# Two conditioning bursts in a row at the head of each pair, from two row buffers, in the first MLP

## The chip, the cores and the metric

The kernel runs on one core of one Trainium2 chip. The time is that of the device in microseconds, for the whole kernel; the number given for a kernel is the median of its runs. "Span" is the time from the first to the last instruction of one profiled execution.

## The reference

The kernel computes one inference step of a two-layer decoder trunk, in float32, for 256 prompt tokens and 8 x 8 sample tokens (320 token columns in all), with a model width of 2048. A layer is a mixer (attention with an RG-LRU in layer 0, a gated short convolution in layer 1) and a squared-ReLU MLP. Each of the four sublayers is modulated by its own conditioning vectors:

```python
def ada_modulate(c, w, b):
    m = jax.nn.silu(c) @ w + b
    shift, scale, gate = jnp.split(m[:, None, :], 3, axis=-1)
    return shift, scale, gate

def sq_relu_mlp(h, w1, w2):
    return jnp.square(jax.nn.relu(h @ w1)) @ w2
...
    shift, scale, gate = ada_modulate(c, W["ada_mlp_w"][layer], W["ada_mlp_b"][layer])
    h = modulated_norm(x, W["norm_mlp"][layer], shift, scale)
    x = x + gate * sq_relu_mlp(h, W["mlp_w1"][layer], W["mlp_w2"][layer])
```

W1 is 2048 x 8192 and W2 is 8192 x 2048; the conditioning matrices are 2048 x 6144 each and meet only nine rows of c. They are read from HBM once, as all weights are.

## The kernel before

Activations stay in SBUF, transposed: a tile is 128 channels x 320 tokens. Every large product is done with three float32r matmuls for each weight tile: a weight chunk (512 rows x 256 columns, 512 KB) is loaded into one of four slots of `raw` by SyncE (SP, `load`, L372), ScalarE copies it into `w_hi` (`split`, L588), VectorE subtracts that from it into `w_lo` (L966), and TensorE multiplies hi by hi, hi by lo and lo by hi (`mul` in `pair`; all its matmuls are recorded at L1656). A chunk is 24 matmuls. A pair is four chunks, which make two output tiles of 128 channels; pairs alternate between two PSUM banks. `w_hi` and `w_lo` have four slots too.

Three waits couple the chunks. Load k waits for `lo_ready` to reach k - 3, that is until chunk k - 4, the one that held its raw slot, has been split. The split of chunk k waits for `chunk_used` to reach k - 3, that is until chunk k - 4 has been multiplied. TensorE waits for `lo_ready` of its own chunk. So load k leaves when chunk k - 8 has been multiplied and chunk k - 4 split behind it. SP issues its DMAs in program order, and each waits in SP's queue behind those ahead of it.

The first MLP (layer 0) works in four blocks of 2048 hidden columns. A block has 8 pairs with W1 (h in, u out; the "column phase") and 8 pairs with W2 (u in, added to x). Between the chunks TensorE also works through conditioning matrices that later sublayers need, one "row" (128 rows x 2048 columns, 1 MB) at a time: a burst (`part_tile`) is four products of a 128 x 32 tile `cs` with a quarter of the row each, on four strips of the array, recorded as eight MATMULs of 128 x 512. In the five first turns of a block (a turn is two pairs: four turns with W1, one with W2) `turn_with_part` puts a burst ahead of chunks 0 and 2 of each pair, 4 to a turn and 80 in all. On SP's side the function of the same name issues, four times a turn, one row and two chunk loads:

```python
for n in range(4):
    sp.wait_ge(narrow_used, KN.now)
    sp.dma_start(narrow_row, ada_rows(ADA[a], row + P * n, part)).then_inc(narrow_in, 16)
    KN.up()
    for src in sources[2 * n:2 * n + 2]:
        load(src)
```

There is one row buffer, `narrow_row` (the tile `narrow`, L420 is its DMA), and `narrow_used` counts the bursts done, so a row is loaded when every burst before it is done. The first four chunks of a turn have been issued by the turn before, so the eight loads of a turn are those of its chunks 4 to 11. ScalarE and VectorE take the four splits of a pair and then that pair's output work (`relu` and square in the column phase, `residual` with W2), four chunks ahead of TensorE. The order of the DMAs and of the matmuls is written out by hand; only SP, ScalarE and VectorE use loops.

Of the kernel before, what the change touches and what calls it, by code (L numbers as in the profile page):

```python
# [13 lines left out]
P = 128  # L14
D = 2048
# [12 lines left out]
SLOTS = 4  # L28
COLS = 256
# [92 lines left out]
@contextmanager  # L122
def looped(eng, lo, hi, per):

    if hi - lo == 1:
        yield lo
        return
    before = [(t, t.base, t.off) for t in per]
    with eng.Fori(lo, hi) as i:
        for t, base, off in before:  # L130
            t.base, t.off = base + i * per[t], off - lo * per[t]
        yield i
    for t, base, off in before:
        added = t.off - (off - lo * per[t])
        assert added == per[t], f"a turn adds {added}, not {per[t]}"
        t.base, t.off = base, off + (hi - lo) * per[t]


def trunk_kernel(nc, A, O):
    with ExitStack() as ctx:  # L140
# [9 lines left out]
        def at(name, offset, shape, dt=F32):  # L150
            return nc.alloc_sbuf_tensor_at(name, shape, dt, offset=offset)

        def new(name, shape, dt=F32):
            return at(name, region(4 * int(np.prod(shape[1:]))), shape, dt)

        def sem(name):
            return ctx.enter_context(nc.semaphore(name))
# [5 lines left out]
        h_hi = at("h_hi", RH, [P, KT, T], F32R)  # L163
        h_lo = at("h_lo", RH + KT * TILE, [P, KT, T], F32R)
        RU = region(2 * KT * TILE)
        u_hi = at("u_hi", RU, [P, KT, T], F32R)
        u_lo = at("u_lo", RU + KT * TILE, [P, KT, T], F32R)
# [13 lines left out]
        RXP = region(4 * LT * (3 + SEQ))  # L181
# [2 lines left out]
        xl_s = at("xl_s", RXS, [P, LT, NB, 3 + DS])  # L184
        c_p = at("c_p", RXP, [P, 2, 2 + SEQ])
        c_s = at("c_s", RXS, [P, 2, NB, 2 + DS])
        h0 = new("h0", [P, LT, NB])
        sc_hist = new("sc_hist", [P, KT, NB, 2])
        lam4 = at("lam4", RH + 32768, [1, 4 * DH])
# [105 lines left out]
        wide_in = [sem(f"wide_in{s}") for s in range(WIDE)]  # L295
        first_in = [sem(f"first_in{s}") for s in range(FIRST)]
        first_used = sem("first_used")
        narrow_in = sem("narrow_in")
        wide_used, narrow_used = sems("wide_used narrow_used")
        amp_ready = sems("amp_ready")  # L300
        in_id, in_tab, in_far, in_c, in_rows = sems("in_id in_tab in_far in_c in_rows")
# [33 lines left out]
        def slab(W, row, col):  # L335

            def at_chunk(s):
                return W[row + 512 * s:row + 512 * (s + 1), bass.ds(col, COLS)].rearrange("(k p) n -> p k n", p=P)
            return at_chunk
# [9 lines left out]
        def ada_rows(W, row, part):  # L349

            return W[bass.ds(row, P), bass.ds(part * D, D)]
# [12 lines left out]
        def _(sp):  # L364
# [22 lines left out]
            def ada_wide(a, part):  # L387

                for n in range(KT):
# [3 lines left out]
                    sp.dma_start(wide_later[:, slot], ada_rows(ADA[a], P * n, part)).then_inc(wide_in[slot], 16)  # L393
                    KW.up()

            def ada_narrow(a, g, tiles):

                if not (isinstance(KN.now, int) and KN.now == 0):
                    sp.wait_ge(narrow_used, KN.now)
                sp.dma_start(narrow[:, :, :], ada_burst(ADA[a], tiles[0], g * GCOLS)).then_inc(narrow_in, 16)  # L400
                KN.up()
# [11 lines left out]
            def turn_with_part(src1, a, part, row, after):  # L413

                sources = [src1(s) for s in range(SLOTS)]
                if after is not None:
                    sources += [after(s) for s in range(SLOTS)]
# [6 lines that stand above are left out]
# [46 lines left out]
            def mlp_weights(layer):  # L470
                return A["mlp_w1"][layer], A["mlp_w2"][layer].rearrange("(b s k p) n -> b s p k n", b=BLOCKS, s=SLOTS, p=P)

            def inward(W2, b, j):
                return lambda s: W2[bass.ds(b, 1), s, :, :, bass.ds(j * COLS, COLS)].rearrange("o p k n -> p (o k) n")
# [8 lines left out]
            def feed_with_ada(b, a, part, after):  # L483

                W1, W2 = mlp_weights(0)
                with looped(sp, 0, 3, {K: 8, KN: 4}) as j:
                    turn_with_part(slab(W1, 0, b * D + j * (2 * COLS) + COLS), a, part, j * (4 * P),
                                   slab(W1, 0, b * D + (j + 1) * (2 * COLS)))
                turn_with_part(slab(W1, 0, b * D + 7 * COLS), a, part, 12 * P, inward(W2, b, 0))
                turn_with_part(inward(W2, b, 1), 2, 2, b * (4 * P), inward(W2, b, 2))  # L490
                with looped(sp, 3, KT // 2, {K: 4}) as j:
                    load_quad(inward(W2, b, j))
                if after is not None:
                    load_quad(slab(W1, 0, after))
# [1156 lines left out]
        def _(pe):  # L1651
# [6 lines left out]
            def pair(r, hi, lo, inputs=None, free=None, count=G, before=None, between=None):  # L1658

                pe.wait_ge(*(free or (pair_free, G.now + 1)))  # L1660
                for s in range(SLOTS):
                    slot = K.off % SLOTS
                    if before is not None:
                        before(s)
                    pe.wait_ge(lo_ready, K.now + 1)
                    for kk in range(4):
                        k = 4 * s + kk
                        if inputs is not None:
                            inputs(s, kk)
                        for m in range(2):  # L1670
                            out, cols = mm[:, r, m, 0:T], slice(P * m, P * m + P)
                            mul(out, w_hi[:, slot, kk, cols], hi[:, k, :], k == 0, False)
                            mul(out, w_hi[:, slot, kk, cols], lo[:, k, :], False, False)
                            ins = mul(out, w_lo[:, slot, kk, cols], hi[:, k, :], False, k == KT - 1)
                    ins.then_inc(chunk_used, 1)
                    K.up()
                    if between is not None:
                        between(s)
                count.up()
# [36 lines left out]
            def ada_wide():  # L1716
# [5 lines left out]
                part_tile(acc, k, wide_later[:, slot]).then_inc(wide_used, 1)  # L1722
                KW.up()

            def ada_part(bank, k):

                pe.wait_ge(narrow_in, KN.now * 16 + 16)
                part_tile(bank, k, narrow_row).then_inc(narrow_used, 1)
                KN.up()
# [21 lines left out]
            def turn_with_part(hi, lo, bank, first, inputs=None, free=(None, None), count=G, after=None):  # L1751

                def burst(first):
                    return lambda s: ada_part(bank, first + s // 2) if s % 2 == 0 else None

                pair(0, hi, lo, inputs, free[0], count, before=burst(first))
                pair(1, hi, lo, None, free[1]() if free[1] else None, count, before=burst(first + 2), between=after)

            def turn_with_ada(hi, lo, inputs=None, free=(None, None), count=G, after=None):

# [7 lines left out]
            def h_inputs(count):  # L1768

                def wait(s, kk):  # L1770
                    if s == 0 and kk < 3:
                        pe.wait_ge(h_ready, count + kk + 1)
                    elif kk == 0:
                        pe.wait_ge(h_ready, count + s + 3)
                return wait
# [32 lines left out]
            def turn(out, in_, rows=P):  # L1808
                return nc.tensor.transpose(out, in_, const[0:rows, 0:rows])  # L1809
# [256 lines left out]
            def u_block():  # L2066

                base, off = UB.base, UB.off
                UB.up(8)
                return lambda s, kk: pe.wait_ge(u_ready, base + (off + 2 * s + 2)) if kk == 0 else None  # L2070

            def mlp_with_parts(count):

                for b in range(BLOCKS):
                    pe.wait_ge(ada_turned, b + 4)
                    turn_with_part(h_hi, h_lo, acc, 0, h_inputs(count),
                                   ((pair_free, G.now + 1), lambda: (pair_free, G.now + 2)), R)
                    for i in range(1, 4):
                        turn_with_part(h_hi, h_lo, acc, 4 * i, None,
                                       ((relu_out, R.now - 1), lambda: (relu_out, R.now - 1)), R)  # L2080
                    relu = R.now
                    turn_with_part(u_hi, u_lo, acc_gate, 4 * b, u_block(),
                                   ((relu_out, relu - 1), lambda: (relu_out, relu)))
                    with looped(pe, 1, 4, {K: 8, G: 2}):
                        for r in range(2):
                            pair(r, u_hi, u_lo)
# [13 lines left out]
                            pair(r, u_hi, u_lo)  # L2100

            UB = Tally()
            pe.wait_ge(l_row, 1)
            norm()
            mlp_with_parts(10)
# [67 lines left out]
```

## Time and profile before

| | |
|---|---|
| median of 3 runs | 3166.12 us (3164.52 to 3168.07) |
| the profiled execution | 3169.29 us, span 3167.6 us |
| TensorE busy | 3061.3 us, 97% of the span |
| VectorE, ScalarE, GpSimd busy | 1480.2, 1084.5, 29.7 us |
| DMA | 624.90 MB, mean 197 GB/s |
| mean granted TensorE clock | 0.982 |

The first MLP goes from about 751 to 1758 us of the span. Busy time of TensorE is the union of its matmuls' records; matmuls overlap (one of 128 x 320 is recorded with 0.31 us), so the distance between starts tells what one costs. Times in the rows are microseconds from the start of the span.

### The profile page before, as it was taken

The numbers are of one execution on the slowest core, as the hardware profiler recorded it, in microseconds if no ns is written. First come the engines' busy times: TensorE is split into PE (matmuls) and PEld (weight loads), VectorE is DVE, ScalarE is ACT, GpSimd is POOL, SyncE is SP. The second block draws the span as 40 slices with busy tenths as digits, with TensorE's granted clock in tenths as the row PEclk, the third lists the DMA queues.
The fourth block names the chain that finished last, engine by engine and source line by source line (L and its number), as shares of the span: only waits on it lengthen the run. The fifth ranks groups of instructions, "written<-read, shape, count | busy, mean of one in ns | idle before, by whom it ended". The sixth has DMA issues, their size and how long they took to land.

```text
span 3167.6 us, 53269 instructions
## 1 busy us (share of the span) xinstructions
PE 3061.3 (97%) x21011; PEld 2818.3 (89%) x21011; DVE 1480.2 (47%) x2057; ACT 1084.5 (34%) x1309; POOL 29.7 (1%) x55
## 2 busy tenths in 40 slices
PE   7999987799999999999999999999999999999998
PEld 4888853598899899889889899999899999999998
DVE  3556544355344344334445644455544444444443
ACT  3334443234332332332332433333432333332332
POOL 0000000000000000000000000000000000000000
PEclk9999998899999999999999999999999999999999
DMA  9987789545765765775774344444444444444443
GB/s 329 335 274 239 240 345 390 221 142 178 251 216 181 263 227 172 252 247 160 245 262 150 123 150 145 152 148 147 125 151 147 144 149 150 143 151 142 147 152 106
DMA packets 451959, 624.90 MB, mean 197 GB/s; under 512 B 16960, under 2 KB 402753, under 8 KB 433028
## 3 DMA queue, kind: packets, MB, share of 16 engines
q1 hardware_dynamic: 443776, 595.65, 56.9%
q0 software_dynamic: 6112, 22.84, 1.9%
q10 hardware_dynamic: 1926, 4.24, 0.4%
q8 instruction: 119, 1.95, 0.3%
q14 instruction: 26, 0.21, 0.0%
HBM read 617.13 MB, written 5.54 MB: 197 GB/s over the span
## 4 chain that ended last, share of the span: by engine, by line
PE 92%; DMA 3%; DVE 2%; issue 2%; ACT 1%; POOL 0%; POOLq 0%; SPq 0%; ACTq 0%; DVEq 0%
PE mm L1656 86%; PE aux L1656 5%; DMA wide_later<-in_ada_mlp_w 2%; DMA wide_first<-in_ada_mix_w 1%; PE mm L1809 1%; DVE tmp L1047 1%; DVE h_lo L1073 0%; DMA kpage<-in_cache_k 0%; DVE tmp L1063 0%; DVE tmp L1066 0%; PE aux L2027 0%; DVE w_lo L966 0%; PE aux L1809 0%; ACT x_sq_b L661 0%; POOLq L542 0%
## 5 line engine op out<-in xcount | busy, mean ns | idle before, releaser
L966 DVE TENSOR_TENSOR w_lo<-raw,w_hi 128x1024 fp32r<-128x1024 f32 x752 | 919.4, 1225 | 1327.4 <-ACT w_hi L588 1325.8
L588 ACT ACTIVATE w_hi<-raw 128x1024 fp32r<-128x1024 f32 x752 | 795.1, 1059 | 1704.8 <-PE mm L1656 1704.8
L1656 PE MATMUL mm<-h_hi,w_hi 128*128 128x320 f32 x3712 | 1170.3, 315 | 30.6 <-DVE h_lo L1073 17.1
L1656 PE MATMUL mm<-h_hi,w_lo 128*128 128x320 f32 x3712 | 1154.7, 311 | 0.0
L1656 PE MATMUL mm<-h_lo,w_hi 128*128 128x320 f32 x3712 | 1154.7, 311 | 0.0
L1656 PEld LDWEIGHTS mm<-h_hi,w_hi 128*128 128x128 f32 x3712 | 704.0, 190 | 131.1 <-issue 102.2
L1656 PE MATMUL mm<-u_hi,w_hi 128*128 128x320 f32 x2304 | 713.7, 310 | 0.0
L1656 PE MATMUL mm<-u_hi,w_lo 128*128 128x320 f32 x2304 | 711.9, 309 | 0.0
L1656 PE MATMUL mm<-u_lo,w_hi 128*128 128x320 f32 x2304 | 711.9, 309 | 0.0
L1656 PEld LDWEIGHTS mm<-h_lo,w_hi 128*128 128x128 f32 x3712 | 704.9, 190 | 0.1
L1656 PEld LDWEIGHTS mm<-h_hi,w_lo 128*128 128x128 f32 x3712 | 704.3, 190 | 0.0
L1656 PEld LDWEIGHTS mm<-u_hi,w_hi 128*128 128x128 f32 x2304 | 432.5, 188 | 13.4 <-issue 13.4
L1656 PEld LDWEIGHTS mm<-u_lo,w_hi 128*128 128x128 f32 x2304 | 432.5, 188 | 0.0
L1656 PEld LDWEIGHTS mm<-u_hi,w_lo 128*128 128x128 f32 x2304 | 432.5, 188 | 0.0
L1656 PE MATMUL aux<-narrow,cs 128*32 128x512 f32 x792 | 112.3, 607 | 0.3 <-DMA narrow<-in_ada_mix_w 0.3
L1302 DVE TENSOR_TENSOR u_lo<-mtmp,u_hi 128x640 f32 x64 | 52.8, 826 | 67.0 <-ACT u_hi L730 67.0
L730 ACT ACTIVATE u_hi<-mtmp 128x640 f32 x64 | 47.3, 739 | 98.5 <-DVE mtmp L1299 98.5
L1237 DVE SCALAR_TENSOR_TENSOR xT<-mm,mod,xT 128x256 f32 (+1 forms) x160 | 69.4, 475 | 0.0
L1656 PE MATMUL aux<-wide_later,cs 128*32 128x512 f32 x384 | 55.7, 654 | 13.7 <-DMA wide_later<-in_ada_mlp_w 13.6
L1299 DVE TENSOR_TENSOR mtmp<-mtmp 128x640 f32<-128x640 f32 x64 | 52.4, 819 | 0.0
L1656 PE MATMUL aux<-wide_first,cs 128*32 128x512 f32 x232 | 43.3, 657 | 4.9 <-DMA wide_first<-in_ada_mix_w 4.1
L728 ACT ACTIVATE mtmp<-mm 128x640 f32<-128x640 f32 x64 | 44.0, 687 | 0.0
(278 smaller groups left out, 1063.4 us busy)
## 6 DMA issues: line engine op xcount, KB each, us to landing
raw<-in_mlp_w SPq DMA_DIRECT2D x512, 512.0 KB, 3.7
narrow<-in_ada_mlp_w SPq DMA_DIRECT2D x64, 1024.0 KB, 5.0
raw<-in_w_in_odd SPq DMA_DIRECT2D x96, 512.0 KB, 3.8
raw<-in_w_in_even SPq DMA_DIRECT2D x80, 512.0 KB, 6.5
narrow<-in_ada_mix_w SPq DMA_DIRECT2D x40, 1024.0 KB, 5.0
wide_later<-in_ada_mlp_w SPq DMA_DIRECT2D x32, 1024.0 KB, 9.8
wide_first<-in_ada_mix_w SPq DMA_DIRECT2D x58, 512.0 KB, 8.4
raw<-in_w_out_even SPq DMA_DIRECT2D x32, 512.0 KB, 3.6
```

The costliest lines, as they stand in the source:

```text
L588: fn(w_hi[:, slot], raw[:, slot], ACT.Copy).then_inc(hi_ready, 1)
L728: fn(mtmp[:, r], mm[:, r, :, 0:T], ACT.Relu).then_inc(relu_out, 1)
L730: fn(u_hi[:, bass.ds(j, 2), :], mtmp[:, r], ACT.Copy).then_inc(u_hi_ready, 1)
L966: v.tensor_tensor(w_lo[:, slot], raw[:, slot], w_hi[:, slot].bitcast(F32), ALU.subtract).then_inc(lo_ready, 1)
L1047: v.tensor_tensor(tmp4[:, first // 4 % 2, first % 4:first % 4 + count], xT[:, first:first + count, :], rstd[:, :].unsqueeze(1).broadcast_t ...
L1237: ins = v.scalar_tensor_tensor(x, mm[:, r, m, 0:SEQ], g, x, ALU.mult, ALU.add)
L1299: v.tensor_tensor(mtmp[:, r], mtmp[:, r], mtmp[:, r], ALU.mult).then_inc(u_val, 1)
L1302: v.tensor_tensor(u_lo[:, bass.ds(j, 2), :], mtmp[:, r], u_hi[:, bass.ds(j, 2), :].bitcast(F32), ALU.subtract).then_inc(u_ready, 1)
L1656: return nc.tensor.matmul(out, lhsT, rhs, start=first, stop=last)
L1809: return nc.tensor.transpose(out, in_, const[0:rows, 0:rows])
```

## The change

In the first MLP the bursts of a pair stand together ahead of its chunk 0, instead of one ahead of chunk 0 and one ahead of chunk 2. The first of the two reads `narrow_row`, the second a new buffer, `second_row`, of 8 KB a partition in the place of `xl_p` (whose readers are in the mixer before, and which the next mixer uses again for `c_p`), with a semaphore of its own. A row load now waits until all bursts but the last one ahead of it are done (`KN.now - 1`). The order of rows and chunk loads in SP's queue stays the same. Everything outside the first MLP is unchanged.

```diff
+        second_row = at("second_row", RXP, [P, D])[:, :]
...
-        narrow_in = sem("narrow_in")
+        narrow_in, second_in = sem("narrow_in"), sem("second_in")
...
+            def part_rows(W1_sources, a, part, row):
+
+                for n in range(4):
+                    sp.wait_ge(narrow_used, KN.now - 1)
+                    into, landed_in = ((narrow_row, narrow_in), (second_row, second_in))[n % 2]
+                    sp.dma_start(into, ada_rows(ADA[a], row + P * n, part)).then_inc(landed_in, 16)
+                    KN.up()
+                    for src in W1_sources[2 * n:2 * n + 2]:
+                        load(src)
...
-                    turn_with_part(slab(W1, 0, b * D + j * (2 * COLS) + COLS), a, part, j * (4 * P),
-                                   slab(W1, 0, b * D + (j + 1) * (2 * COLS)))
-                turn_with_part(slab(W1, 0, b * D + 7 * COLS), a, part, 12 * P, inward(W2, b, 0))
-                turn_with_part(inward(W2, b, 1), 2, 2, b * (4 * P), inward(W2, b, 2))
+                    turn(slab(W1, 0, b * D + j * (2 * COLS) + COLS), slab(W1, 0, b * D + (j + 1) * (2 * COLS)),
+                         a, part, j * (4 * P))
+                turn(slab(W1, 0, b * D + 7 * COLS), inward(W2, b, 0), a, part, 12 * P)
+                turn(inward(W2, b, 1), inward(W2, b, 2), 2, 2, b * (4 * P))
...
+            def ada_two(bank, k):
+
+                for n in range(2):
+                    pe.wait_ge((narrow_in, second_in)[n], 16 * (IN[n] + 1))
+                    part_tile(bank, k + n, (narrow_row, second_row)[n]).then_inc(narrow_used, 1)
+                    IN[n] += 1
...
+            def turn_with_two(hi, lo, bank, first, inputs=None, free=(None, None), count=G):
+
+                def burst(first):
+                    return lambda s: ada_two(bank, first) if s == 0 else None
+
+                pair(0, hi, lo, inputs, free[0], count, before=burst(first))
+                pair(1, hi, lo, None, free[1]() if free[1] else None, count, before=burst(first + 2))
...
-                    turn_with_part(h_hi, h_lo, acc, 0, h_inputs(count),
-                                   ((pair_free, G.now + 1), lambda: (pair_free, G.now + 2)), R)
+                    turn_with_two(h_hi, h_lo, acc, 0, h_inputs(count),
+                                  ((pair_free, G.now + 1), lambda: (pair_free, G.now + 2)), R)
```

The other calls in `mlp_with_parts` change in the same way.

## Rows read from the trace of the kernel before

**Rows 1.** The page: the chain that ended last, by engine.

```profile
PE 92%; DMA 3%; DVE 2%; issue 2%; ACT 1%; POOL 0%; POOLq 0%; SPq 0%; ACTq 0%; DVEq 0%
```

**Rows 2.** Busy time by window: late in the mixer, and a column phase.

```profile
core 0: us, PE busy (x) PEld busy (x) DVE busy (x) ACT busy (x) POOL busy (x), PEclk, DMA share, GB/s
560.00:640.00 80.00, 60.41 (x640) 42.20 (x639) 32.08 (x84) 23.51 (x51) 6.31 (x12) 0.84 0.54 205
1010.65:1134.05 123.40, 123.40 (x841) 107.93 (x841) 48.87 (x48) 41.17 (x45) 0.00 (x0) 1.00 0.76 256
```

**Rows 3.** Timeline of TensorE around a burst: start, duration, what, count.

```profile
1025.80 0.31 PE L1656 MATMUL mm<-h_hi,w_lo 128*128 128x320 f32 x1
1026.04 1.06 PE L1656 MATMUL aux<-narrow,cs 128*32 128x512 f32 x8
1027.03 0.41 PE L1656 MATMUL mm<-h_hi,w_hi 128*128 128x320 f32 x1
1027.28 0.30 PE L1656 MATMUL mm<-h_lo,w_hi 128*128 128x320 f32 x1
...
1030.65 0.31 PE L1656 MATMUL mm<-h_hi,w_hi 128*128 128x320 f32 x1
...
1034.26 0.64 PE L1656 MATMUL aux<-narrow,cs 128*32 128x512 f32 x4
```

**Rows 4.** Timeline of TensorE in the opening: sixteen burst matmuls together.

```profile
92.78 0.31 PE L1656 MATMUL mm<-h_hi,w_lo 128*128 128x320 f32 x1
93.02 0.62 PE L1656 MATMUL aux<-wide_first,cs 128*32 128x512 f32 x2
...
94.87 0.42 PE L1656 MATMUL mm<-h_hi,w_hi 128*128 128x320 f32 x1
95.12 0.31 PE L1656 MATMUL mm<-h_lo,w_hi 128*128 128x320 f32 x1
```

**Rows 5.** Timeline of SP's queue in the column phase: a row, two chunk loads.

```profile
1019.16 0.35 SPq L420 DMA_DIRECT2D narrow<-in_ada_mlp_w  x1
1019.82 0.99 SPq L372 DMA_DIRECT2D raw<-in_mlp_w  x2
```

**Rows 6.** Timelines of ScalarE, VectorE and SP around two splits.

```profile
1030.85 1.06 ACT L588 ACTIVATE w_hi<-raw 128x1024 fp32r<-128x1024 f32 x1 [0.72 <-PE mm L1656]
1031.94 1.23 DVE L966 TENSOR_TENSOR w_lo<-raw,w_hi 128x1024 fp32r<-128x1024 f32 x1 [0.80 <-ACT w_hi L588]
1003.74 1.23 DVE L966 TENSOR_TENSOR w_lo<-raw,w_hi 128x1024 fp32r<-128x1024 f32 x1 [2.29 <-ACT w_hi L588]
1005.13 0.37 SPq L372 DMA_DIRECT2D raw<-in_mlp_w  x1
```

**Rows 7.** A row issued behind a raw load, twice; landings of 75 rows.

```profile
737.41 0.37 SPq L372 DMA_DIRECT2D raw<-in_mlp_w  x1
738.15 0.36 SPq L420 DMA_DIRECT2D narrow<-in_ada_mix_w  x1
...
narrow<-in_ada_mix_w SPq DMA_DIRECT2D x1, 1024.0 KB, 5.4
...
1496.18 0.37 SPq L372 DMA_DIRECT2D raw<-in_mlp_w  x1
1497.07 0.34 SPq L420 DMA_DIRECT2D narrow<-in_ada_mlp_w  x1
...
narrow<-in_ada_mlp_w SPq DMA_DIRECT2D x1, 1024.0 KB, 5.7
...
DMA to landing us min/median/max: 4.8/5.0/7.4
```

**Rows 8.** Timelines of TensorE, VectorE and SP in the MLP's first turn.

```profile
768.64 0.64 PE L1656 MATMUL aux<-narrow,cs 128*32 128x512 f32 x4
...
777.02 1.06 PE L1656 MATMUL aux<-narrow,cs 128*32 128x512 f32 x8
...
772.27 3.65 DVE L966 TENSOR_TENSOR w_lo<-raw,w_hi 128x1024 fp32r<-128x1024 f32 x3
...
773.68 1.83 SPq L372 DMA_DIRECT2D raw<-in_mlp_w  x2
```

More of the change, by code:

```diff
@@ L485, in feed_with_ada, with turn @@
                 W1, W2 = mlp_weights(0)
+                def turn(first, second, *where):
+                    part_rows([f(s) for f in (first, second) for s in range(SLOTS)], *where)
                 with looped(sp, 0, 3, {K: 8, KN: 4}) as j:
-                    turn_with_part(slab(W1, 0, b * D + j * (2 * COLS) + COLS), a, part, j * (4 * P),
-                                   slab(W1, 0, b * D + (j + 1) * (2 * COLS)))
-                turn_with_part(slab(W1, 0, b * D + 7 * COLS), a, part, 12 * P, inward(W2, b, 0))
-                turn_with_part(inward(W2, b, 1), 2, 2, b * (4 * P), inward(W2, b, 2))
+                    turn(slab(W1, 0, b * D + j * (2 * COLS) + COLS), slab(W1, 0, b * D + (j + 1) * (2 * COLS)),
+                         a, part, j * (4 * P))
+                turn(slab(W1, 0, b * D + 7 * COLS), inward(W2, b, 0), a, part, 12 * P)
+                turn(inward(W2, b, 1), inward(W2, b, 2), 2, 2, b * (4 * P))
                 with looped(sp, 3, KT // 2, {K: 4}) as j:
@@ L2075, in mlp_with_parts @@
                     pe.wait_ge(ada_turned, b + 4)
-                    turn_with_part(h_hi, h_lo, acc, 0, h_inputs(count),
-                                   ((pair_free, G.now + 1), lambda: (pair_free, G.now + 2)), R)
+                    turn_with_two(h_hi, h_lo, acc, 0, h_inputs(count),
+                                  ((pair_free, G.now + 1), lambda: (pair_free, G.now + 2)), R)
                     for i in range(1, 4):
-                        turn_with_part(h_hi, h_lo, acc, 4 * i, None,
-                                       ((relu_out, R.now - 1), lambda: (relu_out, R.now - 1)), R)
+                        turn_with_two(h_hi, h_lo, acc, 4 * i, None,
+                                      ((relu_out, R.now - 1), lambda: (relu_out, R.now - 1)), R)
                     relu = R.now
-                    turn_with_part(u_hi, u_lo, acc_gate, 4 * b, u_block(),
-                                   ((relu_out, relu - 1), lambda: (relu_out, relu)))
+                    turn_with_two(u_hi, u_lo, acc_gate, 4 * b, u_block(),
+                                  ((relu_out, relu - 1), lambda: (relu_out, relu)))
                     with looped(pe, 1, 4, {K: 8, G: 2}):
@@ L2102, in _ @@
             UB = Tally()
+            IN = [KN.now, 0]
             pe.wait_ge(l_row, 1)
```

## The prediction

> **What bounds the kernel.** I read the page first, for who sets the end. The chain that ended last is TensorE for 92% of the span [rows 1], so a change counts only by what it adds to or takes from TensorE's own sequence. Next the windows: in a column phase of the first MLP (1010.65 to 1134.05) TensorE is busy for all of 123.40 us at a granted clock of 1.00, while the DMA engines are busy for 0.76 of it and move 256 GB/s [rows 2]. So TensorE waits for nothing there now. Then TensorE's timeline, for what one burst costs, and the timelines of SyncE, ScalarE and VectorE, for when the row that a burst needs can be on its way. I count the chunks of a turn from 0 to 7; a pair is four chunks, and the heads are chunks 0 and 4.
>
> **What a burst costs now.** The last matmul before a burst starts at 1025.80, the burst's eight at 1026.04, the next chunk's first matmul at 1027.03 and its second at 1027.28 [rows 3]. The burst itself takes 0.99. Plain matmuls follow each other every 0.147 (23 of the 24 of chunk 1027.03, less the first step of 0.25, reach to 1030.65). So a burst adds 1.23 - 0.15 on the way in and through, and 0.10 on the way out: 1.19. A half pair, from one burst to the next, is 1034.26 - 1026.04 = 8.22, or 8.227 as the mean of the 15 in the 123.40 us of [rows 2]; a pair of four chunks is 16.45.
>
> **What two in a row cost.** The trace has no two row bursts between chunks, but in the opening twice as many burst matmuls stand together: from the last plain matmul at 92.78 to the next at 94.87 is 2.09, again with 0.25 to the one after it [rows 4]. Two bursts apart take 2 x 1.19 = 2.38; together 2.09 - 0.15 + 0.10 = 2.04. One entry, drain and exit less: 0.34. There is one such merge a pair, 4 blocks x 5 turns x 2 pairs = 40, so 13 to 14 us less, if both rows lie in the buffers when TensorE comes to the head. The number of burst matmuls, row bytes and waits stays as it is; the new buffer lies over xl_p, whose last use is before this MLP, so it costs nothing.
>
> **When the second row is there.** This decides the sign. SP's order does not change: row 0, loads 4 and 5, row 1, loads 6 and 7, row 2, loads 8 and 9, row 3, loads 10 and 11. What changes is the wait ahead of a row. Before, rows 1 and 3 wait for the burst just done at chunk 0 or 4, and are wanted two chunks later; SP's row goes out first and its two chunk loads behind it (1019.16, then 1019.82 [rows 5]), it lands in a median of 5.0 [rows 7], and 8.22 - 1.34 = 6.9 are there for it (SP issued at 1019.16 for the burst at 1026.04). After, the wait of row 3 (for burst 1) is long met, but the row stands in SP's queue behind load 9. Load 9 waits until chunk 5 has been split, since it reuses that raw slot, and the split of chunk 5 waits for chunk 1 to be used, since it reuses that slot of w_hi. So row 3 can't leave before chunk 2 has begun and a split is done, and it is wanted at chunk 4. Row 1 stands in the same way behind load 5. Rows 0 and 2 have twice the time and aren't late.
>
> From the first matmul s of a chunk without a burst ahead: it is 1030.65, w_hi starts at 1030.85 and w_lo ends at 1031.94 + 1.23 = 1033.17 [rows 3, 6], that is s + 2.52. SP issues the raw load 0.16 after the end of w_lo (1003.74 + 1.23 to 1005.13 [rows 6]): s + 2.68. The row follows some 0.65 later, the step between two issues in [rows 5], and moves behind half its size in raw. The nearest rows are the places where a row was issued right behind a raw load: 737.41 and 738.15 with 5.4 to landing, so 6.1 after the raw issue; 1496.18 and 1497.07 with 5.7, so 6.6 [rows 7]. (Two more such places give 6.7 and 8.9, with longer steps between the issues.) I take 6.35, since the step will be short as in the first but some rows land late: up to 7.4 where the median is 5.0 [rows 7]. The second burst can start at s + 2.68 + 6.35 + 0.04 (from a landing to the matmul that waits for it, as the chain has it in the mixer) = s + 9.07.
>
> Without a wait it would start at s + 7.04 (48 matmuls of 0.147) + 0.09 (way in) + 0.86 (half of the growth from one burst of 0.99 to 1.85 for two, 94.87 - 93.02 [rows 4]) = s + 7.99. So TensorE waits 1.1 us between the two bursts of a head. The pair then lasts 3.62 + 3.52 to s, 9.07 to the second burst, and 0.99 for it: 17.20 against 16.45. **Each pair gets 0.75 longer, not 0.34 shorter.** Bounds by the rows: 6.1 gives +0.50 a pair, 6.6 gives +1.00. The same holds in the turn of W2, where VectorE's residual work stands at the heads and not where chunk 5 is split.
>
> A page would put it elsewhere. The Trainium skill (DMA: Bandwidth & Descriptors, Anatomy of one DMA) fits a transfer as 2.0 us plus its bytes at 436 GB/s, for loads issued from GpSimd. An estimate from that fit for raw and row together is 5.6 after the raw issue, which makes a pair 16.45, no change. The trace speaks against it: a row alone lands after 5.0 [rows 7] where the fit has 4.4.
>
> **The first turn.** At the first head nothing is late: the norm keeps TensorE until h is ready, load 5 was issued by 745, long before, and both bursts of that head lie in the norm's wait. But the norm also delays the splits of chunks 4 to 6: VectorE does them in one go from 772.27, SP issues loads 8 and 9 at 773.68 and 774.8, and row 3 leaves at about 775.6 [rows 8]. Behind two raw loads it lands at 780.6 (5.0) to 782.6; I take 782. TensorE, which leaves out the burst at 768.64, is at the head by 775.7 and gets on at 783, where before it was there at 777.02 + 0.99 = 778.0 [rows 8]. That is +5 (3.6 to 5.6).
>
> **The sum.** 40 heads: the first free, the second +5, 38 x 0.75 = 28.5; together +33.5, against the profiled execution's own 3169.3 (span 3167.6 and 1.7 around it): 3202.8. That execution is 3.2 above the median of the three runs, 3166.1, so the forecast is 3166.1 + 33.5 = 3199.6, rounded 3199. The bounds: 38 x 0.50 + 4 = +23 and 38 x 1.00 + 6 = +44, so 3189 to 3210.
>
> **The rivals.**
> (a) Faster: the second row is hidden, and what is left is the merge. 40 x 0.34 = 13.6, and the second burst of the first head goes into the norm's wait, 0.85 more: 3166.1 - 14.4 = 3152. For it: DMA is busy 0.76 [rows 2], so bandwidth is there. It decides from where raw and row together land within 5.3 of the raw issue (7.99 - 2.68); no row shows less than 6.1. Chance 0.08.
> (b) No change to be measured: the row overlaps the raw load more than it did at 738.15, and lands 5.5 to 5.8 after the raw issue, the wait eating just what the merge gives. 38 x 0 + 4.5 gives 3170. Chance 0.09. The page's fit would be this case.
> (c) Worse than forecast: TensorE, which now stands still for 1 us in 17, is granted a lower clock. Where it stood still for a quarter of the time the grant was 0.84 [rows 2]. If 0.95 were granted over the some 680 us of the turns, that is 34 us more: 3233. Against it: TensorE would still be busy for 94% of each pair. Chance 0.05.
> The forecast has the remaining 0.78. What a measurement of this kernel can tell from no change is about 0.2%, 6 us. Faster 0.08, same 0.09, slower 0.83.
>
> **Range.** The forecast's own is 3189 to 3210. To hold 8 in 10 I reach down to (b), 3169, and up to 3211.
>
> **What would show it.** In the profile after: TensorE's burst rows narrow and second_row next to each other at each head; an idle time of about 1 us ahead of the second_row matmuls, ended by the DMA of second_row, 39 times; pairs of 17.2 in the chain; issues of second_row right behind a raw load, 5.5 to 6 to landing, while those of narrow leave earlier than they need; clock 1.00 as before; nothing changed before 750, and the second MLP only shifted. The step of the first head shows as 5 us lost by 783. The prediction is wrong if second_row lands before TensorE has done the first burst, if the raw load ahead of it leaves before the split that I put ahead of it, or if the merged bursts cost more than 2.04.

## The result, and the profile after

The changed kernel takes 3220.98 us (median of 4 runs, 3216.62 to 3231.18) against 3166.43 for the kernel before: a ratio of 1.0177, 95% interval 1.0164 to 1.019. That is 54.6 us slower. The sign and the mechanism are as forecast, the size isn't: 33.5 was forecast, and the time lies 10 us above the range. The profiled execution is the slowest of the four, 3231.18, with a span of 3229.5, so 61.9 us are to be found in its trace.

The page after. First the shares of the engines, the chain that ended last (by engine and by line, two lines) and the group of the second bursts (count | busy, mean ns | idle time ahead of them and its releaser):

```profile
PE 3070.7 (95%) x21011; PEld 2825.3 (87%) x21011; DVE 1480.7 (46%) x2057; ACT 1085.0 (34%) x1309; POOL 29.8 (1%) x55
...
PE 80%; DMA 10%; DVE 4%; issue 2%; ACT 2%; SPq 1%; POOL 0%; POOLq 0%; DVEq 0%; ACTq 0%
PE mm L1671 75%; DMA second_row<-in_ada_mlp_w 5%; PE aux L1671 4%; DMA second_row<-in_ada_mix_w 3%; DVE w_lo L981 2%; DMA wide_later<-in_ada_mlp_w 1%; ACT w_hi L603 1%; DMA wide_first<-in_ada_mix_w 1%; PE mm L1839 1%; SPq L373 1%; DVE tmp L1062 1%; DVE h_lo L1088 0%; DMA kpage<-in_cache_k 0%; DVE tmp L1078 0%; DVE tmp L1081 0%
...
L1671 PE MATMUL aux<-second_row,cs 128*32 128x512 f32 x256 | 37.5, 661 | 45.7 <-DMA second_row<-in_ada_mlp_w 33.2
```

Before, TensorE held 92% of the chain [rows 1]; now it holds 80%, and the chain goes through the second row's DMA and what stands ahead of that DMA: SP's queue, w_lo and w_hi. The DMA queues move the same 624.90 MB as before, at 193 GB/s in place of 197: the row's transfer is not more work, it is late.

An ordinary head, in TensorE's timeline (to be set against [rows 3]), then SP's queue and VectorE's split ahead of it, and the two transfers with their time to landing:

```profile
1593.21 1.06 PE L1671 MATMUL aux<-narrow,cs 128*32 128x512 f32 x8
1595.23 1.06 PE L1671 MATMUL aux<-second_row,cs 128*32 128x512 f32 x8 [0.96 <-DMA second_row<-in_ada_mlp_w]
1596.22 0.41 PE L1671 MATMUL mm<-h_hi,w_hi 128*128 128x320 f32 x1
...
1610.50 0.64 PE L1671 MATMUL aux<-narrow,cs 128*32 128x512 f32 x4
```
```profile
1587.37 1.23 DVE L981 TENSOR_TENSOR w_lo<-raw,w_hi 128x1024 fp32r<-128x1024 f32 x1 [2.29 <-ACT w_hi L603]
...
1588.75 0.37 SPq L373 DMA_DIRECT2D raw<-in_mlp_w  x1
1589.39 0.34 SPq L402 DMA_DIRECT2D second_row<-in_ada_mlp_w  x1
...
second_row<-in_ada_mlp_w SPq DMA_DIRECT2D x1, 1024.0 KB, 5.8
```

The load leaves 0.15 after the end of w_lo (1587.37 + 1.23), the row 0.64 behind it, and it lands 6.4 after the load's issue, at 1595.2. TensorE has been at the head since 1593.21 and starts the second burst 0.04 after the landing. The pair lasts 1610.50 - 1593.21 = 17.29; 17.20 was forecast.

A late head, in the same view; then the windows before the wait ends, behind it and later (length, busy times, PEclk, DMA share, GB/s):

```profile
1627.75 1.07 PE L1671 MATMUL aux<-narrow,cs 128*32 128x512 f32 x8
1632.47 1.94 PE L1671 MATMUL aux<-second_row,cs 128*32 128x512 f32 x8 [3.65 <-DMA second_row<-in_ada_mlp_w]
1634.33 0.63 PE L1671 MATMUL mm<-h_hi,w_hi 128*128 128x320 f32 x1
1634.77 0.47 PE L1671 MATMUL mm<-h_lo,w_hi 128*128 128x320 f32 x1
1635.03 0.47 PE L1671 MATMUL mm<-h_hi,w_lo 128*128 128x320 f32 x1
```
```profile
1627.50:1632.40 4.90, 1.31 (x11) 0.21 (x9) 2.36 (x3) 2.38 (x3) 0.00 (x0) 0.93 0.85 270
1632.47:1638.40 5.93, 5.93 (x23) 4.27 (x24) 0.35 (x1) 0.00 (x0) 0.00 (x0) 0.50 0.70 259
1638.69:1644.00 5.31, 5.31 (x39) 5.31 (x38) 1.23 (x1) 1.48 (x2) 0.00 (x0) 1.00 0.06 13
```

This row landed 8.5 after its issue, not 5.8. TensorE stood still for 3.65 us, and then the granted clock was 0.50, the lower of its two levels (1.2 GHz): the burst takes 1.86 to the next matmul in place of 0.99, plain matmuls step by 0.27 in place of 0.147, until 1638.5. This pair lasts 22.77.

**The balance** of the 61.9 us, from the starts of the 80 bursts in TensorE's timeline. The second burst starts 0.88 after the first where its row is there (as in e2 below, which never waits). At 39 heads, all but the first, it starts later: at 27 of them 1.86 after, on the mean, and at 12 between 2.2 and 5.7. All that is over 0.88 sums to 60.1. Behind eight of these 12 the clock fell, after stops of 1.89 to 4.65 us; what their pairs last beyond the wait, 1.4 to 2.8 each, sums to 15.3. Merging gives back 39 x (16.453 - 16.127) = 12.7, the pair of the kernel before less that of e2. Together +62.7, 0.8 more than the 61.9; that rest isn't assigned.

### The profile page after: what moved, and what is told of

The parts are those of the page before. It is cut to its first block, busy times and chain, and to the rows that moved or that the text cites. A ratio compares the mean times of both kernels' runs of the same rounds, so it can differ in the third digit from the quotient of the medians.

```text
span 3229.5 us, 53269 instructions
## 1 busy us (share of the span) xinstructions
PE 3070.7 (95%) x21011; PEld 2825.3 (87%) x21011; DVE 1480.7 (46%) x2057; ACT 1085.0 (34%) x1309; POOL 29.8 (1%) x55
## 2 busy tenths in 40 slices
DMA packets 451959, 624.90 MB, mean 193 GB/s; under 512 B 16960, under 2 KB 402753, under 8 KB 433028
## 4 chain that ended last, share of the span: by engine, by line
PE 80%; DMA 10%; DVE 4%; issue 2%; ACT 2%; SPq 1%; POOL 0%; POOLq 0%; DVEq 0%; ACTq 0%
PE mm L1671 75%; DMA second_row<-in_ada_mlp_w 5%; PE aux L1671 4%; DMA second_row<-in_ada_mix_w 3%; DVE w_lo L981 2%; DMA wide_later<-in_ada_mlp_w 1%; ACT w_hi L603 1%; DMA wide_first<-in_ada_mix_w 1%; PE mm L1839 1%; SPq L373 1%; DVE tmp L1062 1%; DVE h_lo L1088 0%; DMA kpage<-in_cache_k 0%; DVE tmp L1078 0%; DVE tmp L1081 0%
## 5 line engine op out<-in xcount | busy, mean ns | idle before, releaser
L1671 PE MATMUL mm<-h_hi,w_hi 128*128 128x320 f32 x3712 | 1169.6, 315 | 29.2 <-DVE h_lo L1088 16.7
L1671 PE MATMUL aux<-second_row,cs 128*32 128x512 f32 x256 | 37.5, 661 | 45.7 <-DMA second_row<-in_ada_mlp_w 33.2
L1671 PE MATMUL aux<-narrow,cs 128*32 128x512 f32 x536 | 79.6, 611 | 0.3 <-DMA narrow<-in_ada_mix_w 0.3
```

Source lines behind the costliest of these rows:

```text
L1671: return nc.tensor.matmul(out, lhsT, rhs, start=first, stop=last)
```

## The experiments

Each is the changed kernel with an edit. Its ratio is to runs of the kernel before on the same chip.

**1. The row one load earlier (e1), both rows ahead of all loads (e2).** Only the order in SP's queue changes.

```diff
-                for n in range(4):
+                for n, (lo, hi) in enumerate(((0, 1), (1, 4), (4, 5), (5, 8))):   # e1
+                for n, (lo, hi) in enumerate(((0, 0), (0, 4), (4, 4), (4, 8))):   # e2
...
-                    for src in W1_sources[2 * n:2 * n + 2]:
+                    for src in W1_sources[lo:hi]:
                         load(src)
```

> The changed kernel, but in SyncE's queue rows 1 and 3 stand one load earlier, behind loads 4 and 8 instead of 5 and 9. If the loss comes from the row standing behind a load that waits for the split of chunk 1 (or 5), the row now leaves one chunk (3.5 us) earlier and lands some 2.5 us before it is wanted: the waits of about 2.0 us from the first to the second burst shrink to 0.86, the pair lasts 16.1, and what is left is the merge, 40 x 0.34 less, with some 3 us lost at the second head, where loads are late after the norm: about 3155 us. Rival, that two bursts together or the second buffer itself cost time: it stays near 3215. Rival, that the DMA engines have no room for it: between the two.

> The changed kernel with both rows of a head issued together, ahead of the four chunk loads of a pair. By the theory of the queue no row is late, the second head neither: 3166 - 40 x 0.34 - 0.85 = 3152 us, in all heads 1.85 us from the first burst to the next chunk. Rival, that 2 MB at once hold back the chunk loads: waits of TensorE for w_lo appear, and the time is above 3160. Rival, that merging saves nothing: 3165.

e1: 3156.52 us, ratio 0.997 (0.996 to 0.9979). e2: 3153.01, ratio 0.9957 (0.9944 to 0.9971), 12.5 below the 3165.49 of the runs of before beside it. A head of e2 in TensorE's timeline, and SP's queue of the pair:

```profile
1581.08 1.06 PE L1671 MATMUL aux<-narrow,cs 128*32 128x512 f32 x8
1581.96 1.04 PE L1671 MATMUL aux<-second_row,cs 128*32 128x512 f32 x8
1582.93 0.42 PE L1671 MATMUL mm<-h_hi,w_hi 128*128 128x320 f32 x1
...
1597.20 0.64 PE L1671 MATMUL aux<-narrow,cs 128*32 128x512 f32 x4
```
```profile
1584.31 0.35 SPq L402 DMA_DIRECT2D narrow<-in_ada_mlp_w  x1
1584.71 0.42 SPq L402 DMA_DIRECT2D second_row<-in_ada_mlp_w  x1
1589.09 10.99 SPq L373 DMA_DIRECT2D raw<-in_mlp_w  x4
```

Two bursts take 1582.93 - 1581.08 = 1.85, as in the opening [rows 4], and the pair 16.12 (16.13 on the mean of the heads). Both rows of the next head have left 12 us before it. So the merge is worth what was forecast of it, and the change loses by the place of row 1 and row 3 in the queue against the burst that needs them. In e1, 4 of 39 heads still wait, 0.4 to 2.2 us each; in e2 none does.

**2. The bursts apart again, with everything else of the change (e3), and together at chunk 2 (e4).** `ada_one` is one burst of `ada_two`, with that burst's own buffer and semaphore.

```diff
-                    return lambda s: ada_two(bank, first) if s == 0 else None
+                    return lambda s: ada_one(bank, first + s // 2, s // 2) if s % 2 == 0 else None   # e3
+                    return lambda s: ada_two(bank, first) if s == 2 else None                        # e4
```

> The changed kernel with its two buffers, its semaphores and its order in SyncE's queue, but the bursts stand apart again, ahead of chunks 0 and 2 of a pair. Row 1 leaves as late as in the changed kernel but is wanted two chunks later. By the theory that only the place of the second burst against its row's landing costs: the time of the kernel before, 3166 us, with no wait for a row. Rival, that the shared place in memory, the late issue or the other wait cost by themselves: well above 3170.

> The changed kernel with both bursts together ahead of chunk 2 of each pair instead of chunk 0, with SyncE's order unchanged. Row 1 then has two chunks (7 us) more. By the theory: no wait for a row, the merge's gain of 40 x 0.34 = 13.6 us, less 1.2 because the norm hides no burst any more: 3154 us. Rival, that standing together costs: above 3166.

e3: 3162.98 us, ratio 0.9993 (0.9984 to 1.0002), no change that can be told. So the buffer in the place of xl_p, the semaphores, the wait and the late issue cost nothing that can be told as long as the burst that needs the row stands two chunks later. e4: 3152.75, ratio 0.996 (0.9945 to 0.9975): standing together at a place where the row is there gives the whole gain, with SP's order untouched. Neither kernel's waits name a row's DMA in this MLP.

**3. Half of each second row (e5), and the row ahead of its load (e7).** These divide the row's lateness.

```diff
+                    width = (D, D // 2)[n % 2]                                        # e5
+                    sp.dma_start(into[:, 0:width], ADA[a][bass.ds(row + P * n, P), bass.ds(part * D, width)]).then_inc(landed_in, 16)
...
+                for n, (lo, hi) in enumerate(((0, 1), (1, 4), (4, 5), (5, 8))):       # e7
+                    if n % 2:
+                        sp.wait_ge(lo_ready, K.now - 3)
+                    else:
+                        sp.wait_ge(narrow_used, KN.now - 1)
```

> The changed kernel with half of each second row: its DMA brings 128 rows x 1024 columns (512 KB), and the burst multiplies those columns twice, so the conditioning values that come from the second rows are not the reference's; TensorE's matmuls keep their number and size. If the row is late because it moves behind a raw load and takes its own 1 MB, it lands about 1.4 us earlier, so the second burst starts some 0.86 after the first at most heads and the pair lasts 16.1: 40 x 0.34 less, with some us left at late landings and at the second head, about 3157 us. Rival, that a late start alone sets it (the fixed part of a transfer): the wait stays above 0.5 us and the time above 3180.

> The changed kernel, but rows 1 and 3 change places with the load that stands ahead of them (5 and 9) and wait for the same split as that load, so a row leaves at the moment at which load 5 left. This divides the lateness into the wait for the split (kept) and the standing behind a raw load (0.65 us of issue and that load's transfer, gone). By the theory the row lands 5.0 after an issue at s + 2.68, so it is there at s + 7.7, just before s + 8.0: no wait at most heads, waits of 1 to 3 us where a row lands late, some 3 us at the second head; 3166 - 12.7 + about 10 = 3163 us. Rival, that the split's wait alone makes it late: nearly the changed kernel's 3215.

e5: 3166.7 us, ratio 1.0005 (0.9995 to 1.0014). e7: 3166.07, ratio 0.9998 (0.9984 to 1.0012). Time to landing of second_row (min/median/max), of e5 and then of e7; after the change it was 5.4/5.8/8.5:

```profile
DMA to landing us min/median/max: 4.1/4.8/7.0
```
```profile
DMA to landing us min/median/max: 4.8/5.0/7.4
```

Either edit takes about 54 of the 54.6 us away. What waits are left just eat the merge's gain, so both are as fast as the kernel before. In e7 the row leaves at the moment at which load 5 left, right behind the split, and lands after 5.0. In its profiled execution, one of the faster ones (3158.68), the landing is 0.2 to 0.65 ahead of the second burst at 26 of 39 heads. The margin is so thin that a late landing still costs: the bursts start 3.2 apart at the second head and 3.1 at another (1253.77 to 1256.86). That kernel's runs spread over 15 us (3155.86 to 3171.09). So the split's wait alone puts the row at the edge, and the 0.65 of issue and the raw transfer ahead put it past it. I had expected e5 10 us lower: halving the row brought it in 1.0 earlier, not 1.4, which leaves small waits, mostly under 0.5 us, at 24 of 39 heads. (The half that e5 leaves out is half of every second row's conditioning weights, so its values aren't the reference's.)

**4. What a long wait costs beside itself (e6, e8).** e6 moves rows 1 and 3 behind loads 6 and 10. e8 does the same and fills the wait.

```diff
+                for n, (lo, hi) in enumerate(((0, 3), (3, 4), (4, 7), (7, 8))):       # e6, e8
...
+                    if n:                                                             # e8, in ada_two
+                        for _ in range(4):
+                            for m in range(4):
+                                mul(mm[32 * m:32 * m + 32, 2, 0, :], cs[:, k, :], const[:, 0:512], True, True)
                     pe.wait_ge((narrow_in, second_in)[n], 16 * (IN[n] + 1))
```

> The changed kernel with rows 1 and 3 one load later in SyncE's queue, behind loads 6 and 10, so that each leaves one chunk (3.52 us) later. This asks what a longer wait costs beside itself. The theory: a wait of over 3.5 us brings TensorE's granted clock down, as at the nine heads of the changed kernel that waited so long, each some 2 us more after the wait; then every pair lasts 17.2 + 3.5 + 2.0 = 22.7 and the kernel 3166 + 40 x 6.3 = 3415 us, with the clock at 0.5 in stretches behind each head. Rival, that these heads had the late landing and the lost time from one cause outside TensorE: a pair of 20.8, 3166 + 40 x 4.3 = 3340 us, with the clock at 1.00.

> The kernel with rows 1 and 3 behind loads 6 and 10 (3430 us), and between the two bursts of a head four more bursts' worth of matmuls that read a constant and write a PSUM bank that nobody reads in this stage (32 MATMULs of 128 x 512, some 3.4 us), so that TensorE stands still only for about 1.2 us of the 4.6. They are extra work and change no output. If it is TensorE's standing still that brings the granted clock down, the clock stays at 1.00, the second burst still starts 5.5 to 5.7 after the first, and a pair lasts 20.9 in place of 23.2: about 3340 us, 90 less than without the extra work. Rival, that the clock fell from some other cause that comes with the late rows: the extra matmuls run at the low clock too, and the time is 3430 or more.

e6: 3430.29 us, ratio 1.083 (1.0802 to 1.0858). e8: 3372.64, ratio 1.0654 (1.0629 to 1.0679), 58 less with 1280 matmul instructions more. A head of each in TensorE's timeline, and the windows from one head to the next:

```profile
1525.83 1.07 PE L1671 MATMUL aux<-narrow,cs 128*32 128x512 f32 x8
1531.63 1.08 PE L1671 MATMUL aux<-second_row,cs 128*32 128x512 f32 x4 [4.73 <-DMA second_row<-in_ada_mlp_w]
...
1525.83:1549.41 23.58, 18.85 (x114) 16.08 (x113) 6.46 (x6) 5.56 (x6) 0.00 (x0) 0.86 0.51 179
```
```profile
1057.68 1.06 PE L1671 MATMUL aux<-narrow,cs 128*32 128x512 f32 x8
1058.56 3.62 PE L1671 MATMUL mm<-const,cs 128*32 128x512 f32 x32
1063.23 1.06 PE L1671 MATMUL aux<-second_row,cs 128*32 128x512 f32 x8 [1.06 <-DMA second_row<-in_ada_mlp_w]
...
1057.68:1078.50 20.82, 19.76 (x145) 15.43 (x145) 6.08 (x8) 4.24 (x4) 0.00 (x0) 1.00 0.59 202
```

The second burst starts 5.80 after the first in e6's head and 5.55 after it in e8's. In e6 the pair lasts 23.58 with the clock at 0.86 over it; in e8 20.82 with 1.00. In e6 TensorE stands still for 4.0 to 5.5 us at each of the 39 heads, the clock falls behind all 39, and a pair loses 2.3 on the mean beyond the wait. With the wait filled, the clock falls behind 12 heads in e8, where the row came later still (at 1142 TensorE stood still for 1.99 us behind the extra matmuls); there the loss is 1.56, and at the others 0.02. So the clock falls because TensorE stands still, and not from a cause that comes with the late rows. e8 lies 33 us above its expectation: its rows land later than in e6 (a median of 6.0 and up to 8.1 after the issue, against 5.8 and 6.8), which makes some 17 us of wait, and the 12 falls make some 19. The expectation of e6 has one thing wrong: not nine heads of the changed kernel waited over 3.5 us. The clock fell behind eight, and only three of those stops were over 3.5.

For stops of about 2 us the length alone doesn't say whether the clock falls. Two second bursts, one of the changed kernel and one of e1, each with the window behind it:

```profile
1029.61 1.06 PE L1671 MATMUL aux<-second_row,cs 128*32 128x512 f32 x8 [1.89 <-DMA second_row<-in_ada_mlp_w]
1029.60:1034.50 4.90, 4.89 (x24) 4.06 (x25) 0.72 (x3) 0.00 (x0) 0.00 (x0) 0.65 0.83 291
```
```profile
1259.45 1.06 PE L1671 MATMUL aux<-second_row,cs 128*32 128x512 f32 x8 [2.01 <-DMA second_row<-in_ada_mlp_w]
1259.00:1265.00 6.00, 5.55 (x39) 4.71 (x40) 1.04 (x4) 0.73 (x1) 0.00 (x0) 1.00 0.83 303
```

A stop of 1.89 brought the clock down, one of 2.01 didn't. At the heads of the changed kernel, e1, e5, e7 and e8, no stop of up to 1.5 us did, every one of 2.3 us or more did, and of those between some did and some didn't.

## Why the prediction was right or wrong

**The cost of two bursts together: right.** 0.34 less for a merge was forecast; e2's pairs say 16.13 against 16.45, 0.33. 39 merges count, not 40, see below. (The 1.19 of a burst alone was not measured by itself.) The 0.86 that the prediction calls half of a growth is the whole of it, 1.85 - 0.99; as a distance between the two starts it is right, 0.88 in the trace.

**When the row leaves and when TensorE wants it: right.** The load at s + 2.68, the row 0.65 behind it, wanted at s + 7.99. The ordinary head has 0.15, 0.64, and a start distance of 0.88 without a wait. The pairs of the 27 heads without a late landing last 16.7 to 17.4, with a median of 17.2: the forecast 17.20.

**The landing: the step that failed.** "I take 6.35, since the step will be short as in the first but some rows land late." The median of the 39 is 6.43 after the raw issue, but the mean is 6.80, and since TensorE waited at every one of the 39 heads, the sum of its waits follows the mean. 12 of 39 heads started the second burst 2.2 to 5.7 after the first. They make all of the 13.7 us by which the waits (60.1) exceed those in the forecast (38 x 1.08, and 5.4 at the second head, make 46.4); the 27 others wait 0.98, a little less than forecast. The rows of before had told it in part. All rows of that MLP together had a mean of 5.1 where the median was 5.0, for all that one took 7.4 [rows 7]. But of the four places where a row followed a load only two went into the 6.35; the four rows took 5.4, 5.6, 7.4 and 5.7, a mean of 6.0, and with the step of 0.65 that is 6.7 after the load. In the kernel before, late landings were free: no wait of TensorE there names a row's DMA. The change takes that cover away.

**The clock: the second term, priced at nothing.** The sum has no term for the clock, because TensorE would still be busy for 94% of each pair; rival (c) had it as an even loss that hangs on that share, and gave it 0.05. What happens is that single waits do it: a stop of 1.0 us leaves the clock at 1.00, one of 3.65 us halves it for some 6 us. It is 15.3 us in this execution; e6 and e8 show that the standing still is the cause. Both missed terms hang on the same 12 landings: 13.7 + 15.3 = 29.0, and 33.5 + 29.0 = 62.5 comes near the 61.9 of this execution. That is the slowest of the four; the median lies 21 us above the forecast. The other three have no trace, so that they differ by how many rows land late in each is likely but not shown.

**The first turn: the size near by luck.** TensorE was to be at the second head by 775.7, because the burst at 768.64 falls away. It came at 778.10, 24.48 after the first head, as before (777.02 - 752.55 = 24.47): that burst had lain in the norm's shadow, and e2 waits 0.91 for h_lo in its place. So this merge gives nothing, and the first head's second burst hides there, which gives nothing either. Counted from the first head, TensorE was thus 1.3 later than forecast, which shortens the wait; the row landed 0.7 later, which makes it longer. The wait is 4.65 us, and it costs a fall of the clock too: the pair lasts 23.19, that is 6.7 more than before where 5 was forecast, and 2.2 of it is the clock.

**The rivals.** (a) is what e2 and e4 do, at 3153 and not 3152; no run of the change itself comes near it. (b) wanted the row 5.5 to 5.8 after the load's issue; the trace has a median of 6.43 and a least value of 6.0. The estimate from the Trainium skill (DMA: Bandwidth & Descriptors, Anatomy of one DMA), a fit for loads issued from GpSimd, was 5.6 for load and row together. These loads are issued by SyncE, and the measurement decides.

## What to carry to other kernels

When two uses of loaded data move together, ask of each load what stands ahead of it in its issuer's queue and what that waits for, and move the load with its use: here the same change with both rows ahead of the chunk loads is 0.4% faster than the kernel before, and without that it is 1.8% slower. Price a transfer that loses its cover by the mean and the tail of its landings, not by the median. And a stop of TensorE can cost more than its length: here some stops of 1.7 to 2.3 us did, and all longer ones.

## What the runs showed of the hardware that I had not expected

TensorE's clock: after a stop of 3.65 us the grant was 0.50 for 6 us, and a stop of 1.89 us was enough in one place and one of 2.01 not in another; at the ordinary heads, after stops of about 1 us, it stayed 1.00. Useless matmuls in the wait (3.6 us of them a head) made e8 58 us faster than e6.

Some rows of 1 MB land late: up to 2.4 us behind the median in the kernel before, 2.7 in the changed one and 4.3 in e1. At least 1 us behind it are 6 of 77 rows of this MLP in the kernel before and 7 of 39 second rows in the changed one. Behind the five latest of these 7, the load issued some 2.9 us after the row was late with it: it took 6.4 to 7.0 to land, where 4.2 is usual. What holds them up stays open: it wasn't tried.
